# Two hybrid layers on one core: norm stages prepared between the output projections' slabs, operand handed over tile by tile, weights split two slabs ahead

## The reference

```python
def hybrid_layer(x, c, ...):                       # first layer
    mod = silu(c) @ w_ada + b_ada; shift, scale, gate = split(mod, 3)
    h = rmsnorm(x, pre_g) * (1.0 + scale) + shift
    q, k, v, gate_a, u, gate_p = split(h @ w_in)
    y_a = windowed_gqa(q, k, v, rel_table, sink) * silu(gate_a)
    y_p = multiscale_pool(u, w_pool_grp, pool_scale) * silu(gate_p)
    g_a, g_p = split(sigmoid(h @ w_merge + b_merge))
    o = (g_a * (y_a @ w_br_attn) + g_p * (y_p @ w_br_pool)) @ w_out
    return x + gate * rmsnorm(o, post_g)

for l in range(1):                                 # second layer
    sh1, sc1, g1, sh2, sc2, g2 = split(silu(c) @ w_mod + b_mod, 6)
    h = rms_norm(x, pre) * (1.0 + sc1) + sh1
    y = token_mixer(h, ...)     # rope + sliding window attention, gated linear attention, merge, w_out
    x = x + g1 * rms_norm(y, post)
    h = rms_norm(x, ffn_pre) * (1.0 + sc2) + sh2
    y = conv_ffn(h, w_up, conv_w, conv_b, w_down)  # silu(gate) * val, a causal conv of 3 taps before
    x = x + g2 * rms_norm(y, ffn_post)
```

## Time and profile before

| | |
|---|---|
| Median of 3 runs | 2522.36 us |
| The profiled execution | 2521.72 us |
| Its span | 2519.9 us |
| Its mean granted TensorE clock | 0.951 |
| PE busy | 2312.4 us, 92% |
| DVE busy | 1789.0 us, 71% |
| ACT busy | 1153.7 us, 46% |
| POOL busy | 94.1 us, 4% |
| DMA | 580.67 MB, 230 GB/s in the mean |

### The profile page before, as it was taken

How to read it: one execution, slowest core, us unless ns; L and a number is a source line. 1 busy time by engine, 2 the same in 40 slices (tenths; PEclk the granted TensorE clock), 3 DMA queues, 4 the chain that set the end, 5 groups by cost and what they waited for, 6 DMA issues and landing times.

```text
span 2519.9 us, 32064 instructions
## 1 busy us (share of the span) xinstructions
PE 2312.4 (92%) x12836; PEld 1982.0 (79%) x12836; DVE 1789.0 (71%) x2282; ACT 1153.7 (46%) x1637; POOL 94.1 (4%) x113
## 2 busy tenths in 40 slices
PE   2499999999995889999999999997999999989997
PEld 1388888888784768888888888886888888878886
DVE  6767777779854787777677888646777777764444
ACT  1343455555445345454455455445444444434443
POOL 1000000000000000000011100000000000000000
PEclk8599999999996989999999999998999999999998
DMA  9867778878843757578777788743555555556662
GB/s 380 353 229 271 260 260 286 292 269 308 307 158 120 258 175 259 202 248 293 263 262 256 253 291 306 268 167 117 186 198 184 171 197 184 189 158 188 188 184 80
DMA packets 313032, 580.67 MB, mean 230 GB/s; under 512 B 12187, under 2 KB 105167, under 8 KB 308533
## 3 DMA queue, kind: packets, MB, share of 16 engines
q1 hardware_dynamic: 300224, 535.86, 62.3%
q0 software_dynamic: 11328, 40.26, 4.9%
q10 hardware_dynamic: 1332, 2.51, 0.3%
HBM read 557.61 MB, written 20.97 MB: 230 GB/s over the span
## 4 chain that ended last, share of the span: by engine, by line
PE 60%; DVE 9%; ACT 4%; issue 2%; DMA 0%; DVEq 0%; ACTq 0%
PE gemm L1607 38%; PE gemm L1608 19%; DVE w_lo L985 2%; DVE mod_acc L978 1%; PE extra L1430 1%; ACT w_hi L676 1%; ACT quad_work L676 1%; PE extra L1422 1%; DVE proj L1057 1%; ACT scores L676 0%; ACT operand_main L676 0%; DVE small L1198 0%; DVE scores L1195 0%; DVE proj L1054 0%; PE extra L1516 0%
## 5 line engine op out<-in xcount | busy, mean ns | idle before, releaser
L1607 PE MATMUL gemm<-operand_main,w_hi 128*128 128x512 f32 x4880 | 1740.0, 404 | 72.9 <-issue 26.5
L1608 PE MATMUL gemm<-operand_main,w_lo 128*128 128x256 f32 x4880 | 1329.3, 283 | 0.0
L1607 PEld LDWEIGHTS gemm<-operand_main,w_hi 128*128 128x128 f32 x4880 | 911.9, 191 | 281.0 <-issue 44.3
L985 DVE TENSOR_TENSOR w_lo<-w_stage,w_hi 128x1024 fp32r<-128x1024 f32 (+2 forms) x774 | 876.0, 1160 | 361.1 <-ACT w_hi L676 360.6
L676 ACT ACTIVATE w_hi<-w_stage 128x1024 fp32r<-128x1024 f32 (+2 forms) x776 | 766.3, 1007 | 653.5 <-PE gemm L1608 652.4
L1608 PEld LDWEIGHTS gemm<-operand_main,w_lo 128*128 128x128 f32 x4880 | 934.7, 192 | 30.1
L978 DVE SCALAR_TENSOR_TENSOR mod_acc<-mod_stage,c_silu,mod_acc 128x1024 f32<-128x1024 f32 x224 | 285.4, 1315 | 0.6 <-DMA mod_stage<-in_w_mod 0.6
L676 ACT ACTIVATE low_part<-gemm 128x256 f32<-128x256 f32 x329 | 125.4, 384 | 326.7 <-PE gemm L1607 302.6
L1607 PE MATMUL gemm<-ffn_hidden,w_hi 128*128 128x512 f32 x704 | 249.8, 401 | 9.8 <-issue 9.8
L1608 PE MATMUL gemm<-ffn_hidden,w_lo 128*128 128x256 f32 x704 | 196.1, 282 | 0.0
L1607 PEld LDWEIGHTS gemm<-ffn_hidden,w_hi 128*128 128x128 f32 x704 | 132.5, 190 | 41.7 <-issue 10.1
(11 more groups left out here) (198 smaller groups left out, 1214.5 us busy)
## 6 DMA issues: line engine op xcount, KB each, us to landing
w_stage<-in_w_in SPq DMA_DIRECT2D x128, 1024.0 KB, 6.2
mod_stage<-in_w_mod SPq DMA_DIRECT2D x192, 512.0 KB, 5.6
w_stage<-in_w_up SPq DMA_DIRECT2D x88, 1024.0 KB, 5.0
w_stage<-in_w_down SPq DMA_DIRECT2D x64, 704.0 KB, 4.8
w_stage<-in_w_ada SPq DMA_DIRECT2D x32, 1024.0 KB, 8.0
w_stage<-in_w_merge SPq DMA_DIRECT2D x32, 1024.0 KB, 5.5
w_stage<-in_w_out SPq DMA_DIRECT2D x32, 1024.0 KB, 5.5
mod_stage<-in_w_ada SPq DMA_DIRECT2D x32, 512.0 KB, 6.0
```

Source lines behind the costliest of these rows:

```text
L985: tt(WL[:, s1 % 2, c0:c1], WST[:, s1 % 4, c0:c1], WH[:, s1 % 2, c0:c1].bitcast(F32), ALU.subtract)\
L1607: hi = lambda **kw: mm(bank[:, :], WH[:, s % 2, c0:c0 + P], X_[:, k, :], **kw)
L1608: lo = lambda **kw: mm(bank[:, T:2 * T], WL[:, s % 2, c0:c0 + P], X_[:, k, 0:T], **kw)
```

## The change

The hand-written order stays, with one phase for each output quad instead of segments of several bodies; all gemms and their shapes stay. What differs:

1. **Ring of weights.** `w_stage` has 5 slots and `w_lo` lies in the same bytes: DVE subtracts in place. `w_hi` has 3 slots. Both parts are made two slabs ahead. A slot is loaded again when the gemm five slabs before has ended; hi is made, both halves, when the gemm three slabs before it has ended. TensorE waits for a whole slab.
2. **Evacuation by pairs of tiles.** ACT copies the low halves of two banks straight to the destination, DVE adds the high halves onto it; `low_part` and ACT's small copies (`take_wait`, `k_head`, `v_head`) are gone. In up the conv's taps are done by DVE within the evacuation, after each pair's addition.
3. **Hooks.** In qkvb attn5 of the first of two head pairs stands in slab 3 before the evacuation (it was behind it). Rows of mod: branch1 has 3 in its 4 slabs (2 before), branch2 4 in each 6, out1 2 in each of two phases, out2 none; mod_end 4 comes behind out1's second phase and mod_end 8 behind out2's first.
4. **Norms behind the output projections.** In slab 2 of the next phase of out1, out2 and down ACT squares the quad finished before and scales it by gate times norm weight, and TensorE adds it up (`out_sq`). Behind the last slab only two pairs of tiles are left. The new x is a product with rstd and a sum for each quad; quads 0, 1 and 3 on DVE, quad 2 on POOL.
5. **Operand by tiles.** `prep_h` makes the operand tile by tile (DVE, ACT, DVE); gk, u0 and the first phase of up wait for single tiles, their slabs but the last run chunk by chunk over the tiles.
6. **down.** 4 groups of 4 tiles and 11 slabs instead of 16 groups of one tile; a slab waits only for its quad of the hidden layer.
7. **The end.** x and the scaled output are transposed to token rows in slabs of down (`x_turn`, `o_turn`), the sums of squares are taken by token (`token_sums`, one column), and behind the last slab DVE multiplies by rstd and adds, 128x512 a time.
8. **Start.** SP's fifth row of the first modulation matrix waits until the small vectors and x have landed; the loops over these rows are written out.

```diff
+RAW, HIS, AHEAD = 5, 3, 2
...
-                hooks={**attn_hooks(0, pair[0]), **attn_hooks(4, pair[1])},
-                late={**attn_late(0, pair[0]), **attn_late(4, pair[1])},
+                hooks={**attn(0, pair[0]), **attn(4, pair[1]), 3: [("attn4", pair[0]), ("attn5", pair[0])]},
+                late=[("attn5", pair[1])],
...
+            phases.append(Phase("branch1", i, [Group(A["w_branch_attn"][0], 512 * i, 2, "attn", "merge_a", n=i),
+                                               Group(A["w_branch_pool"][0], 512 * i, 2, "main", "merge_b", n=i)],
+                                mod=(4, 3 * i, 3), pre=[] if i else [("poolmix", 0), ("prep_y", 1)]))
+            phases.append(Phase("out1", i, [Group(A["w_out"][0], 512 * i, 4, "main", "proj", tile=16 + 4 * i)],
+                                hooks={2: [("out_sq", (0, i - 1))]} if i else {}, mod=(4, 12 + 2 * i, 2) if i < 2 else None,
+                                pre=[] if i else [("prep_merged", 0)], post=([], [("mod_end", 4)], [], [("resid", 0)])[i]))
...
+        def mods_behind(ph, s):
+            rows = ph.mod[2] if ph.mod else 0
+            return [r for r in range(rows) if r * len(ph.slabs) // rows == s]
...
+            def free_slot(t):                      # SP, before a load
+                if RAW <= t < MOD0_ROWS + RAW:
+                    sp.wait_ge(mod0_rows, t - RAW + 1)
+                elif t >= MOD0_ROWS + RAW:
+                    sp.wait_ge(slab_used, t - MOD0_ROWS - RAW + 1)
...
+            def split_hi(n):                       # ACT
+                for h, c0, c1 in halves(n):
+                    if h == 0:
+                        act.wait_ge(w_landed[slot_of(n)], landed(n))
+                    if h == 0:
+                        positive(act, slab_used, n - HIS + 1)
+                    activate(WH[:, n % HIS, c0:c1], WST[:, slot_of(n), c0:c1], ACT.Copy).then_inc(hi_made, 1)
...
+                for s, (g, q) in enumerate(ph.slabs):          # DVE
+                    if ph.slab0 + s + AHEAD < len(slabs):
+                        split_lo(ph.slab0 + s + AHEAD)
+                    for h in ph.hooks.get(s, ()):
+                        hook(*h)
+                    for r in mods_behind(ph, s):
+                        mod_row(ph, r)
+                    if q == g.slabs - 1:
+                        evac(g)
...
+                if what == "resid" and k < 2:                  # DVE
+                    norm_rs(norm_of[("resid", k)])
+                    dve.wait_ge(start["resid_in"], 16 * (k + 1))
+                    dve.wait_ge(o_scaled, 5 * k + 5)
+                    for js in ((0, 1), (3,)):
+                        for j in js:
+                            o = PROJ[:, 16 + 4 * j:20 + 4 * j, :]
+                            ins = tt(o, o, RSQ, ALU.mult)
+                        link(ins)
+                        for j in js:
+                            x = PROJ[:, 32 + 4 * j:36 + 4 * j, :]
+                            tt(x, x, PROJ[:, 16 + 4 * j:20 + 4 * j, :], ALU.add).then_inc(new_x, 1)
...
+                    for s in range(KT + 2):                    # DVE, prep_h
+                        if s < KT:
+                            if s >= 8:
+                                dve.wait_ge(op_ready, base + s - 7)
+                            stt(WORK[:, s % 8, :], src[:, src0 + s, :], AFF[:, s:s + 1], RS[:, :], ALU.mult, ALU.mult).then_inc(scaled, 1)
+                        t = s - 2
+                        if t >= 0:
+                            dve.wait_ge(op_hi, base + t + 1)
+                            stt(HL[:, t, T:2 * T], WORK[:, t % 8, :], MODV[:, shift + t:shift + t + 1], HL[:, t, 0:T].bitcast(F32),
+                                ALU.add, ALU.subtract).then_inc(op_ready, 1)
...
+            def gemm(n):                                       # TensorE
+                pe.wait_ge(lo_made, 2 * n + 2)
...
+                if g.operand == "hid":
+                    pe.wait_ge(hid_done, q + 1)
+                for m, kc in order:
+                    k = q * QUAD + kc
+                    if k == 0 and m % 2 == 0 and g.gi:
+                        before = groups[g.gi - 1]
+                        wait_evac(pe, before, min(m // 2 + 1, before.pairs))
+                    if by_tile and m == 0:
+                        pe.wait_ge(op_ready, op_count[name] - 16 + k + 1)
```

More of the change, by code:

```diff
@@ L223, in build @@
         w_in2 = A["w_in_2"][0]
-        gp = lambda c, w=w_in, s=512, tile=None: Group(w, c, s, 4, "main", "proj", tile=c // P if tile is None else tile)
-        attn_hooks = lambda o, a: {o + s: [(f"attn{s + 1}", a)] for s in range(4)}
-        attn_late = lambda o, a: {o + 3: [("attn5", a)]}
-        segs = []
-        segs.append(Segment("u0", 1, [gp(2560)]))
-        segs.append(Segment("u1", 1, [gp(3072)], mod=(2, 2, 0)))
+        phases = []
+        one = lambda c: Group(w_in, c, 4, "main", "proj", tile=c // P)
@@ new lines, in build @@
+        for i in range(3):
+            phases.append(Phase("qkv2", i, [two(512 * i, 4 * i)], mod=(5, 2 * i, 2), post=[("rope", 0)] if i == 2 else []))
+        for i in range(4):
+            pair = [dict(blk=2, kv=i, u=8 + 2 * i + half, pair=2 * i + half) for half in range(2)]
+            phases.append(Phase("qkvb", i, [two(1536 + 1024 * i, 12 + 8 * i), two(2048 + 1024 * i, 16 + 8 * i)],
+                                hooks={**attn(0, pair[0]), **attn(4, pair[1]), 3: [("attn4", pair[0]), ("attn5", pair[0])]},
+                                late=[("attn5", pair[1])],
+                                mod=((5, 6, 5), (5, 11, 5), (6, 0, 4), (6, 4, 4))[i], post=[("mod_end", 5)] if i == 1 else []))
@@ new lines, in build @@
+        for i in range(4):
+            if i == 0:
+                behind = {0: [("ffn_val", 10)], 1: [("ffn_hi", 10)], 2: [("ffn_lo", 10)], **{4 + c: [("x_turn", c)] for c in range(4)}}
+            else:
+                behind = {2: [("out_sq", (2, i - 1))], 4: [("o_turn", i - 1)]}
+            phases.append(Phase("down", i, [Group(A["w_down_2"][0], 512 * i, 11, "hid", "late", tile=4 * i)], hooks=behind,
+                                post=[("resid", 2)] if i == 3 else []))
+        groups, slabs = [], []
@@ new lines, in build @@
+        n_pairs, mods = 0, 0
+        for ph in phases:
+            ph.slab0 = len(slabs)
+            ph.mod0 = mods
+            mods += 2 * ph.mod[2] if ph.mod else 0
+            for g in ph.groups:
+                g.gi = len(groups)
+                groups.append(g)
+                g.pair0, g.full0 = n_pairs, n_pairs - g.gi
+                n_pairs += g.pairs
+            for s, (g, q) in enumerate(ph.slabs):
+                g.last = len(slabs)
+                slabs.append((ph, g, q))
@@ L293, in build @@
+        named = lambda name: [ph for ph in phases if ph.name == name]
+        first = lambda name: named(name)[0]
         MOD0_ROWS = 32
@@ new lines, in _ @@
+                if ph.name in ("out1", "out2", "down") and i == 0:
+                    load_resid({"out1": 0, "out2": 1, "down": 2}[ph.name])
+                if ph.name == "merge":
+                    pool.wait_ge(start["lines_stored"], 16 * HEADS1)
+                    positive(pool, biased, i)
+                    for b in range(2):
+                        at0 = 255 - P * b
+                        pool.dma_start(BIAS[:, b, :], lines[i, at0:at0 + P * (LINE - 1)].rearrange("(q k) -> q k", k=LINE - 1)[:, 0:T])\
+                            .then_inc(bias_landed, 16)
+                    store_gate(0, ph.groups[0])
@@ new lines, in _ @@
+                    pool.wait_ge(gs["sig"], i + 1)
+                    nc.gpsimd.tensor_tensor(OG[:, :, :], OG[:, :, :], VF[:, :, :], ALU.mult).then_inc(gs["gate"], 1)
+                    store_gate(1, ph.groups[1])
+                if ph.name in ("branch1", "branch2"):
+                    blk = int(ph.name[-1]) - 1
+                    if i == 0:
+                        pool.wait_ge(gate_stored, 16 * (8 if blk == 0 else 20))
+                        if blk == 1:
+                            pool.wait_ge(gs["y"], 16)
+                    positive(pool, merge_tiles, 2 * (i + 4 * blk))
+                    for half in range(2):
+                        pool.dma_start(GL[:, half, :, :], gates[blk, 4 * i + 16 * half:4 * i + 16 * half + 4].rearrange("t q n -> q t n"))\
+                            .then_inc(gates_in, 16)
@@ L659, in _ @@
+                for what, k in ph.post:
                     stage(what, k)
@@ L1369, in _ @@
+                for h in ph.late:
+                    hook(*h)
+                for what, k in ph.post:
+                    stage(what, k, ph)
         @block.tensor
```

1181 lines of the change are left out of this document (545 added, 636 removed).

## The result

The changed kernel takes 2561.79 us (median of 4 runs, 2560.45 to 2563.48), the kernel before 2523.04 beside it (2521.14 to 2526.69): ratio 1.0152, 95% interval 1.0135 to 1.017. It is 39 us slower. The forecast was 2546, some 25 us slower, and the time lies in the range. Its profiled execution took 2560.62 us with a span of 2558.5, 38.6 more than before.

The account below looks back on a forecast made before the run. TensorE was taken as the bound, its 2064 us of gemm pairs staying. Terms -18 -16 +35 -11 -18 +18 +27 +9 sum to +26 on 2521.7: 2548, rounded down to 2546; 8-in-10 range 2506 to 2570.

Parts of the forecast that it names:

- The seams: Behind out1 and out2: the way from the last gemm back to steady gemms gets shorter, -18 and -16 us.
- square, sums, root, reciprocal as now: At the seam behind out1, after the new x: these steps take 5.7 us, as in the kernel before.
- What was moved is not gone: Sums of squares and two mod_ends laid between gemms cost in full: about +35 us, between 31 and 40.
- Up to down: Between up and down: a wait per slab replaces TensorE's wait for the whole hidden layer, -11 us.
- the end: Behind the last gemm: 13.2 us instead of 31.0, -18 us, bounds -14 and -20.
- (a): qkvb: attn5 of the first pair before the evacuation makes TensorE wait at gemm 4: +18 us, bounds 9 and 22.
- (b): branch1 and branch2: mod rows in neighbouring slabs delay the evacuation, eight stalls of 3.0 us plus clock: +27, bounds 0 and 40.
- (c): gates2 and attention: later splits lengthen TensorE's waits, +6 and +3, together +9 us, bounds 0 and 15.
- Costed at nothing: Evacuation by pairs, conv in up, in-place lo with five slots, dropped small copies, and the start: 0 us (start -4 to +4).
- rival C: Weight ring starves: loads slip in the branches, 40 slabs late by 1 to 2 us, +40: 2580 us; chance 0.08.
- Rival A: Faster: the new DVE order in qkvb and the branches does no harm, stalls under 17 us: 2500 us; chance 0.22.
- Rival B: Stalls in qkvb and the branches come but half, at 9 and 12: 2524 us, no change; chance 0.14.

Follow-up runs that it names:

- the experiment: Changed kernel with attn5 of each qkvb phase's first head pair moved behind the first group's evacuation: 2542.4 us, ratio 1.0073 to the kernel before.
- the combined one: Changed kernel with mod rows spread, mod_ends in the hole, attn5 and gla7 behind evacuation, new x on DVE, evacuation before mod rows in every phase: 2474.84 us.

## Why the prediction was right, by its own steps

- **The seams, -18 and -16**: measured -15.8 and -12.2. The third slab of qkv2 starts 74.3 behind the last gemm (forecast 72.4); before it was 91.9 and not the 90.1 of the prediction, which gave the slab that starts at 825.36 the full pace, where its first half ran at the low clock (the third slab starts at 833.17). That makes -17.6 up to there, of which the rest of qkv2 gives 2 back. Eight slabs of up end at 78.3 (forecast 74.7). The first gemm came at 28.6, not 25.7. The terms listed up to the first reciprocal add up to 5.2 and not to the 6.3 written; 6.1 were measured, so the listing was short, not the number. The 1.15 for an instruction of 1024 columns is a mean over several shapes; alone it takes 1.22. The new x took 11.3 us (forecast 11.8: the two engines do take turns), but the step "square, sums, root, reciprocal as now" failed: TensorE does the sums of four quads in 9.2 us after its idle time, they can't start before the first pair of quads is through, and from the end of the new x to the end of the second reciprocal it is 9.2 us instead of 5.7. The run on DVE alone took 4.9 us out of the whole:

```profile
786.97 9.24 PE L1419 MATMUL extra<-quad_work,ones 128*128 128x256 f32 x32 [11.35 <-ACT quad_work L657]
```

- **What was moved is not gone, +35**: the phases of out1 and out2 became 11.1 and 8.9 longer (forecast 23 for both), down's hooks cost 9.3 (its 258.2 us less 704 pairs of 0.3535) where 12.6 were said. +29 in all. That the mod_ends cost in full where they were put is shown by the run that lays them into the hole: 10.4 less. This term came 6 under its forecast and the seams gained 6 less than theirs: the two misses cancel, which is luck.
- **Up to down, -11, and the end, -18**: -12 (9.9 for the hole, 2.2 for the slow restart that was in down, a sum from the stage lengths) and -18.1. The end takes 12.9 us (forecast 13.2) and is in the order that was worked out: the eight stores follow DVE's rows.
- **(a), +18**: 21.2 by the experiment. Waits of 4.5, 4.5, 2.3 and 2.3 us, forecast 4.6 and 2.4. The 4 for the clock was too low: 7.6 of the 21.2 are not in these waits, 1.2 of them in shorter waits for scores.
- **(b), +27**: the term that was mis-sized; measured +42.0, beyond its own bound of 40. The mechanism was seen where it was forecast, eight waits before the third slab with DVE waiting for mod_stage just before. But each is 3.9 us and not 3.0: I had first worked out 4.3 and then let the gates' shorter landing talk it down. That is 7 us. Another 6 are in the deduction of "some 9 that these stretches lose now": only about 3 came back, since TensorE's other holes in the branches were 10.9 us before and are 8.1 now. The last 2 are the clock, whose price was nearly right: the same matmuls are busy for 13.7 us longer (lines by stage above), 1.7 a hole, where 1.5 were forecast. The mean granted clock (0.91 and 0.92, from 0.98 and 0.99) would make more of it, since it also counts the time in which TensorE waits. What I hadn't seen at all is that three rows in four slabs are more than one can land in time, so that another order on DVE doesn't free branch1 of all its waits.
- **(c), +9**: gates2 +4.2 of 6, with the wait at 3.9 as worked out (4.0). The step that failed is the count: there are three such holes in gates2 and not four, in the kernel before too. Of the 3 for attention the waits came and the time did not: TensorE's waits for scores in qkvb rose from 7.6 to 10.9, but with attn5 in its old place qkvb is as long as before (225.8 and 225.6), and so is merge. What was gained against it is not shown.
- **Costed at nothing**: the start moved by 1.3 us, up lost nothing, and no load of weights held TensorE up in the branches (rival C; its sum should read 2586, 40 above the forecast). The rows of mod did come late there: DVE stood idle for their landing for 4.9 us in branch1 and 10.2 in branch2. But the conv was hidden by the lead of two slabs, which the prediction didn't say.
- **Rival A** had its point of decision at stalls of (a) and (b) under 17 us; they are 44.7 (31.1 and 13.6). The 45 that the prediction set against them holds the clock and the deduction; its stalls alone are 24 and 14. Rival B is out by the same rows.

## What to carry to other kernels

Price each added item of an engine's queue by what stands right behind it: here some 65 of the 87 us between the changed kernel and the combined one (37 in the branches, 14 in qkvb, 14 in gates2) were in the main an evacuation on which TensorE waits, behind something that had time. A stream through two buffers has a shortest period (consume, issue, land: 7.9 us here, for two half rows), and it has to be laid against the length of the phase before its items are packed more densely. Work moved out of a seam is free only when it goes where TensorE waits anyway; between two gemms it costs its full time and some clock. So the 15.8 us gained at the first seam left 4.5 for its whole stretch, with 11.1 spent between the gemms before it.

## What was not expected of the hardware

- DVE with two operands in SBUF beside such an instruction on POOL: 2.25 and 2.20 us instead of 1.22, POOL 3.37 and 3.20 instead of the 2.64 of the earlier trace rows. Four of DVE's and two of POOL's took 8.9 us, where one after the other they would take 4.9 and 5.3: only 1.3 us of it were side by side. Turns had been forecast; what had not is that a quarter of the work given to POOL makes the step longer than DVE alone, which does all eight in 9.7 us.
- The mean granted clock of a stretch with holes is not the price of its slow restarts. Branch1 and branch2 stood at 0.91 and 0.92, which reads as 24 us of full speed lost where some 4 were before (9% of 120 and 8% of 165, against 2% of 100 and 1% of 143); the matmuls were busy for only 13.7 us longer than before, 1.7 a hole of 3.9 us, as behind the hole of 2.6 in gates2.
